# Attention with two heads on the halves of TensorE's columns and scaling on GpSimd, and a reordered end of each recurrence head

## The reference, cut to what matters

```python
# attention: 8 heads of 64, the tokens as rows of 64; a query sees 8 rows of keys (4 in the short sequence)
s = jnp.einsum('rqhd,rjkhd->hrqjk', qg, kg) * scale + bias       # bias: table by distance, -1e30 outside a 16 wide band
p = jax.nn.softmax(s.reshape(H, rows, GRID_W, kh * GRID_W), axis=-1)
o = jnp.einsum('hrqjk,rjkhd->rqhd', p, vg)

# recurrence: 4 heads of 128, forward and backward, the same for both
k, log_f = (1 - lb) * sigmoid(-z), log(max(lb + (1 - lb) * sigmoid(z), 1e-30))
S[t] = exp(log_f[t]) * S[t-1] + k[t] v[t]^T ;   o[t] = silu(q[t]) S[t]
```

## Time and profile before

| | us |
|---|---|
| median of 3 runs (lowest to highest) | 3038.07 (3037.3 to 3043.27) |
| the profiled execution, its own time | 3038.7 |
| its span | 3036.9 |
| attention, start of the first product to the end of the last copy | 484.7 to 639.2 |
| recurrence, closing products of the four heads begin at | 773.4, 868.9, 962.0, 1043.9 |

### The profile page before, as it was taken

One profiled execution on the slowest core, in us unless ns is written; L12 is line 12 of the kernel. 1 busy time (PEld: TensorE's weight loads), 2 busy tenths in 40 slices (PEclk: granted clock), 3 DMA queues, 4 the chain that ended last, 5 costly groups with the idle time before them and its releaser, 6 DMA issues. The chain is left out here.

```text
span 3036.9 us, 50700 instructions
## 1 busy us (share of the span) xinstructions
PE 2887.0 (95%) x19594; PEld 2707.7 (89%) x19594; DVE 2109.2 (69%) x3534; ACT 1577.8 (52%) x2728; POOL 549.4 (18%) x518
## 2 busy tenths in 40 slices
PE   7999999989988889978999999999999999999997
PEld 5888888978877778858999999999999999999997
DVE  7212224767888576677778877887788778778887
ACT  2111214654455333316666666666666666667774
POOL 2000110014534243311001100110011001102132
PEclk9999999999999989988999999999999999999998
DMA  6478864845545464328878887888788879889894
GB/s 225 157 212 253 271 187 117 237 171 192 193 168 192 141 216 135 125 97 273 255 259 267 266 258 258 268 263 257 256 273 259 257 257 285 262 255 313 273 298 142
DMA packets 534559, 686.64 MB, mean 226 GB/s; under 512 B 18969, under 2 KB 460584, under 8 KB 529200
## 3 DMA queue, kind: packets, MB, share of 16 engines
q1 hardware_dynamic: 514816, 627.96, 63.9%
q0 software_dynamic: 19504, 55.44, 7.0%
HBM read 577.46 MB, written 105.88 MB: 225 GB/s over the span
## 5 line engine op out<-in xcount | busy, mean ns | idle before, releaser
L2581 DVE TENSOR_TENSOR moe_low<-pieces_ring,moe_high 128x1024 fp32r<-128x1024 f32 x768 | 930.4, 1222 | 155.2 <-ACT moe_high L2484 154.5
L2484 ACT ACTIVATE moe_high<-pieces_ring 128x1024 fp32r<-128x1024 f32 x768 | 796.1, 1052 | 16.6 <-PEq L103 16.6
L2431 PE MATMUL moe_down<-moe_hdn,moe_high 128*128 128x320 f32 x1920 | 510.7, 346 | 9.6 <-DVE moe_outT_p L2619 4.3
L2431 PE MATMUL moe_gate<-moe_xT,moe_high 128*128 128x320 f32 x1792 | 480.8, 344 | 0.9 <-DVE moe_xT L2586 0.9
L2431 PE MATMUL moe_up<-moe_xT,moe_high 128*128 128x320 f32 x1792 | 474.0, 340 | 2.4 <-DVE moe_low L2581 2.4
L2432 PE MATMUL moe_down<-moe_hdn,moe_low 128*128 128x160 f32 x1920 | 453.4, 236 | 0.0
L2432 PE MATMUL moe_up<-moe_xT,moe_low 128*128 128x160 f32 x1792 | 423.4, 236 | 0.0
L2432 PE MATMUL moe_gate<-moe_xT,moe_low 128*128 128x160 f32 x1792 | 423.3, 236 | 0.0
L2431 PEld LDWEIGHTS moe_down<-moe_hdn,moe_high 128*128 128x128 f32 x1920 | 361.4, 188 | 17.8 <-DVE moe_hdn L2610 8.3
L2432 PEld LDWEIGHTS moe_down<-moe_hdn,moe_low 128*128 128x128 f32 x1920 | 366.9, 191 | 0.0
L2432 PEld LDWEIGHTS moe_gate<-moe_xT,moe_low 128*128 128x128 f32 x1792 | 343.0, 191 | 0.0
(11 more groups left out here) (344 smaller groups left out, 6075.0 us busy)
## 6 DMA issues: line engine op xcount, KB each, us to landing
pieces_ring<-in_w_gate_e SPq DMA_DIRECT2D x128, 1024.0 KB
pieces_ring<-in_w_up_e SPq DMA_DIRECT2D x128, 1024.0 KB
pieces_ring<-in_w_down_e SPq DMA_DIRECT2D x128, 1024.0 KB
bias_fx<-xs SPq DMA_DIRECT2D x40, 1024.0 KB, 5.3
fr_raw<-in_w_in SPq DMA_DIRECT2D x16, 1024.0 KB, 8.6
ws<-fr_late_split SPq DMA_DIRECT2D x32, 512.0 KB, 4.6
bias_fw<-ws SPq DMA_DIRECT2D x32, 512.0 KB, 8.2
mo_gates<-h SPq DMA_DIRECT2D x20, 512.0 KB, 4.5
```

What stands on the lines that cost most here:

```text
L2431: nc.tensor.matmul(ps[:, 0:2 * TOK], hi, x, start=(first and k == 0), stop=False)
L2484: nc.scalar.activation(high[:, g % HI, cols], ring[:, g % RAW, cols], ACT.Copy)\
L2581: nc.vector.tensor_tensor(low[:, g % HI, cols], ring[:, g % RAW, cols], high[:, g % HI, cols].bitcast(F32), ALU.subtract).then_inc(lo_done, 1)
```

## The change

In the attention, `values` takes both heads of a tile at once: for each chunk a product of 64 columns of `v` for head 0 into rows 0 to 63 of the result, and one for head 1 into rows 64 to 127. The two are addressed to the two halves of the array's columns, and one copy of 128 rows takes both out. The products of a tile are spread over two rounds, half the chunks in each. The scaling by the reciprocal goes from DVE to POOL. The turned tile is held in two buffers and copied in two parts, the first three chunks by ACT and the rest by DVE. `pT` has four slots instead of two. POOL makes the `na_inner` tables of the last two pairs of heads between scalings, and stores there as well. The pipeline is one round deeper.

In the recurrence the closing products wait for A group by group, the last `gather` stands ahead of `run_sums` on DVE, `gates` moves from round 6 to round 7, and in the first three heads the second half fill of the last level goes behind the closing products.

```diff
+                def scale(g):                                     # POOL
+                    keys, n = items[g][5], g % SLOTS
+                    pool.wait_ge(inverted, g + 1)
+                    nc.gpsimd.tensor_scalar(sc[:, n, 0:keys], sc[:, n, 0:keys], inv[:, n:n + 1], None, ALU.mult)\
+                      .then_inc(normed, 1)
+                make_inner(0)
+                make_inner(1)
+                for g in range(G):
+                    scale(g)
+                    pool.wait_ge(normed, g + 1)
+                    hp, n = divmod(g, N)
+                    if n == 2 and 1 <= hp < NA_HEADS // 2 - 1:
+                        make_inner(hp + 1)
+                    if n == 12 and hp >= 1:
+                        store(hp - 1)
...
-                    for c in range(0, keys, P):
-                        last = nc.tensor.matmul(o_ps[g % 2][:, 0:P], v[:, w, k0 + c // P, :], pT[:, g % 2, c:c + P],
-                                                start=(c == 0), stop=(c + P >= keys))
+                    for n in range(*((0, chunks // 2) if half == 0 else (chunks // 2, chunks))):
+                        for u in range(2):
+                            head = slice(u * NA_DIM, (u + 1) * NA_DIM)
+                            last = nc.tensor.matmul(o_ps[slot][head, :], v[:, w, k0 + n, head],
+                                                    pT[:, (2 * pair + u) % SLOTS, n * P:(n + 1) * P],
+                                                    start=(n == 0), stop=(n == chunks - 1))
...
-                for g in range(G + 4):
+                for g in range(G + 5):
                     if g < G:
                         scores(g)
                     if 3 <= g < G + 3:
                         turn(g - 3)
-                    if g >= 4:
-                        values(g - 4)
+                    if g >= 5:
+                        values((g - 5) // 2, (g - 5) % 2)
...
                     if g < G:                                     # DVE
                         bias(g)
-                    if 2 <= g < G + 2:
-                        norm(g - 2)
-                    if g >= 5:
-                        copy_o(g - 5)
+                    if 1 <= g < G + 1:
+                        invert(g - 1)
+                    if 3 <= g < G + 3:
+                        copy_p(g - 3)
+                    if g >= 7 and g % 2:
+                        copy_o((g - 7) // 2)
...
+            if hd + 1 < HG_HEADS:
+                points[-1] = (hd, "closed")
...
-                    pe.wait_ge(a_done, (hd + 1) * NL * NG)
                     pe.wait_ge(s_made, (hd + 1) * NS)
                     for g, (a, count) in enumerate(CHUNK_GROUPS):
+                        pe.wait_ge(a_done, ((hd + 1) * NL - 1) * NG + g + 1)
...
+                    fill((hd, "closed"))
...
-                        if r == 6 and hd + 1 < HG_HEADS:
+                        if r == 7 and hd + 1 < HG_HEADS:
                             gates(hd + 1, 1 - w)
...
+                    gather(R - 2)
                     if hd + 1 < HG_HEADS:
                         run_sums(hd + 1)
-                    gather(R - 2)
```

More of the change, by code:

```diff
@@ L721, in _ @@
-                for g in range(G + 4):
+                    for m, cols in enumerate(parts_of(g)):
+                        if g >= 1:
+                            pe.wait_ge(p_copied[m], g)
+                        for c in range(cols.start, cols.stop, P):
+                            last = nc.tensor.transpose(t_ps[m][:, c - cols.start:c - cols.start + P],
+                                                       sc[:, g % SLOTS, c:c + P], ident[:])
+                        last.then_inc(p_turned[m], 1)
@@ new lines, in values @@
+                def values(pair, half):
+                    hp, _, _, t, k0, keys, row, two = items[2 * pair]
+                    w, slot = hp % 2, pair % 2
+                    if half == 0:
+                        for m in range(2):
+                            pe.wait_ge(p_copied[m], 2 * pair + 2)
+                        if pair % PAIRS == 0:
+                            pe.wait_ge(v_in[w], 16 * (hp // 2 + 1))
+                        if pair >= 2:
+                            pe.wait_ge(o_copied, pair - 1)
+                    chunks = -(-keys // P)
+                    for n in range(*((0, chunks // 2) if half == 0 else (chunks // 2, chunks))):
[4 more added lines that the diff above has]
+                                                    start=(n == 0), stop=(n == chunks - 1))
+                    if half == 1:
+                        last.then_inc(pv_done, 1)
@@ L737, in bias @@
                     if g >= SLOTS:
-                        dve.wait_ge(p_turned, g - SLOTS + 1)
-                    rows = inner[:, 2 * hp + u] if two else table[:, 2 * hp + u, row:row + keys // GRID_W, :]
+                        dve.wait_ge(p_turned[1], g - SLOTS + 1)
+                    rows = inner[:, (2 * hp + u) % HEADS] if two else table[:, 2 * hp + u, row:row + keys // GRID_W, :]
                     nc.vector.tensor_tensor_reduce(
@@ L743, in bias, with invert @@
                         ALU.add, ALU.min, nmax[:, n:n + 1]).then_inc(biased, 1)
-                def norm(g):
-                    keys, n = items[g][5], g % SLOTS
+                def invert(g):
+                    n = g % SLOTS
                     dve.wait_ge(exp_done, g + 1)
[L748 to L752, removed]
```

96 lines of the change are left out of this document (50 added, 46 removed).

## The result

The changed kernel takes 3024.21 us (median of 5 runs, 3022.08 to 3025.53) against 3039.27 us (5 runs, 3037.3 to 3044.64) of the kernel before: ratio 0.9945, 95% interval 0.9931 to 0.9960, faster by 15 us. The forecast was 3001, with a range of 2986 to 3036. The sign is right, and less than half of the gain came.

What follows compares the result with a forecast made beforehand. PE was taken to bound the attention, while in the recurrence neither engine is full. From 3038.7 us, minus 30 (attention) and minus 7 (recurrence), with mixing and experts 0, gave 3001.7, stated as 3001; range 2986 to 3036.

Steps and rivals of the forecast that it cites:

- Value products, minus 35.5 us: Attention, PE: the two heads' products run at once on two column halves, two sharing one 0.111 us slot; minus 35.5 us.
- Switches of shape, taken at 0: Attention, PE: 160 switches between full and half width, two each way per round or fewer, assumed to cost about 0.
- the row of the 32-column transposes: Profile row before the change: 32-column transposes between full-width instructions, read as a switch at about 0.
- upper end of 0.166 us: Attention: if PE empties first, a switch costs a small product's length less its pitch, 0.166 us, 26.6 us in all.
- The forecast's sum for it with overlap, 3028 us: Attention: halves overlap but PE empties at each of 160 switches; 3001.7 + 26.6 = 3028 us.
- the forecast's first rival: Attention: halves overlap, but part of a drain, POOL or the chain through four slots takes over; 137 to 149 us, 3020; chance 0.26.
- Scaling on POOL at 1.0 us: Attention: a scaling of 512 to 576 columns takes about 1.0 us on POOL, ends 0.6 and 1.8; some 76 us for 80.
- 125: Attention's forecast length: 155.3 - 35.5 + 2 (DVE) + 2 (POOL) + 1.5 (pipeline) = 125 us, gain 30.
- DVE and ACT, 94.7 and 36 us: Attention: DVE's busy time falls from 118.2 to 94.7 us, ACT's copies from 47.8 to about 36 us.
- the 2 us for short rounds: Attention: in 16 rounds with 256 keys only DVE needs 1.05 us against PE's 0.93; plus 2 us.
- Recurrence, minus 7: Recurrence: moved gates and freed closing, less the scans' later place, give 1 + 3 + 3 = 7 us over three heads.
- 2 to 3.5 us a head: Recurrence: gain from moving the gates one round later, of which the scans' later place takes 1.5 to 2 us back.

Runs made afterwards that it cites:

- the run in one half: Changed kernel with all value products writing rows 0 to 63, one head's chunks per round, two copies out on DVE: 3053.22 us, ratio 1.0043 to the kernel before.
- The added switches: Changed kernel with the value products of 64 rounds laid in two places, one between the transposes' parts, 124 more changes of shape: 3039.66 us.
- full width: Changed kernel with value products 128 columns wide, one head per round, no overlap and no switch, POOL still scaling: 3032.61 us.
- half the switches: Changed kernel with both halves of a pair's value products in one round, 80 switches instead of 160: 3022.77 us.
- the shared version: Changed kernel with a pair's value products in one round, and scaling of odd items on DVE, even ones on POOL: 3016.01 us.
- no scaling on POOL: Changed kernel with all scaling back on DVE, directly behind the reciprocal: 3018.55 us.
- half of both: Same run as the shared version: changed kernel, value products once per pair, every second item's scaling on DVE: 3016.01 us.

## Why the prediction was right in sign and wrong in size

*Value products, minus 35.5 us: right.* The pitch halved, 32.5 us went from between the instructions, and the run in one half shows that the overlap is what did it.

*Switches of shape, taken at 0: the step that failed.* The forecast took the row of the 32-column transposes, which shows no drain, over its own upper end of 0.166 us. In the trace the borders of the value products cost 30.9 - 11.6 = 19.3 us more, and 3.0 of the 35.5 didn't come between the instructions: 22.3 us for 152 borders, 0.15 us each. The stage as a whole says the same more roughly: 151.1 - 159.6 + 35.5 less 2 to 6.1 for POOL is 21 to 25 us. The added switches gave 0.15 as well, and so does the run in one half, which has switches and no overlap. It stood 181.6 - 163.5 = 18.1 us above full width, with 5.4 us less of other waits (5.0 for POOL and 1.5 for ACT there against 1.1), 23.5 us for 155 changes. So the upper end, a small product's length less its pitch, was nearly the price. The forecast's sum for it with overlap, 3028 us, lies within 4 of the result, and has the switches 4 us too dear. What came is the forecast's first rival, given 0.26: an attention of 137 to 149 us, counted to 640.0, where 146.8 was measured on that scale, by the first of the causes it names, the drain. The Trainium skill has a change of tiling mode drain TensorE (TensorEngine Tiling (Array Packing), Key Properties); the gaps of 0.17 us in this trace agree. The row that the forecast preferred stays what it was, a change at no price, but for 32 columns and transposes; why it was free there wasn't tried, and it was too far from 64 columns and products to carry 160 changes. That a drain is what fills the 0.15 us is argued from its length; shown is that the changes of shape cost it.

*Scaling on POOL at 1.0 us: too low.* It took 1.57 and 1.73 us for 512 and 576 columns, 120 us in sum against 76. The row of a scaling, 583 ns for 127 columns, was no bad start. What failed is the slope, 1.0 ns a column as of a copy: from 256 to 512 columns it measured (1567 - 927) / 256 = 2.5 ns. PE's direct loss stayed small all the same. The weight loads waited 6.1 us for POOL, but 4.1 for DVE's scaling before, so 2 us more, as forecast. The larger effect is the hidden one: with POOL's 129 us under PE's 142, half the switches could go without gain. Nor could 125 have come true. POOL's first scaling starts 3.5 us into the stage, its last ends 8.0 us before the next stage, and between them POOL is busy for 125.2 us. So even switches at no price leave an attention of some 137 us, an estimate from these rows, where the forecast's 125 is 129.3 on the same scale.

*DVE and ACT, 94.7 and 36 us: 89.1 and 35.9.* Near enough; neither held the stage, and the 2 us for short rounds weren't needed: no wait for DVE is longer than 0.2 us.

*Recurrence, minus 7: minus 7.5 in the profile, 7 by the run of it alone.* The sum is right, and by luck, since its split is not. The level-7 wait in the second head (some 5 us forecast, 5.4 measured), closing at once behind the gather (forecast 214.7 us after the recurrence's start, measured 212.1), and PE's wait that moves to the next head's transposes came as described. But the whole gain hangs on the gates: put back, they cost 8.5 us, where the forecast had 2 to 3.5 us a head less what the later scans take. The kernel is then 8.2 us faster than before, what the attention gives alone, so for the gather ahead of the scans and the moved half fill together next to nothing is left; the scans put back cost 1.5 us, not to be told from none, and the half fill wasn't tried alone. The reason in the rows: the next head's first weights, done at 862.1 in the second head, hold PE's transposes at 862.6 whatever closing does before them; taking ACT's copies out of the way gave only 0.5 us a border.

*Left open.* The single steps of the recurrence sum to 10 us and the whole to 7; the difference is about what such runs can tell. What the shared version's 4.9 us without a releaser are isn't known.

## What to carry to other kernels

Narrow products pay if both halves of the columns get work, and each way into and out of the narrow shape is paid, here with 0.15 us on average: eight of these instructions save 0.44 us and lose 0.24 to 0.3. So it should pay to gather many in one place before switching; here that gave nothing while POOL did all the scaling. When work moves to a quiet engine, set its whole sum, at a slope from the same kind of instruction, beside the new time of the engine that it relieves. Test two suspects together and not only one at a time: half the switches gave nothing in the attention, no scaling on POOL 3.8 us, half of both 7.1. In the times that is weaker (1, 5.5 and 7 us, each with some us of doubt), and how the two are combined matters more: half the switches with all scaling on DVE was slower than either alone.

## What the runs showed of the hardware

DVE's scaling of 512 and 576 columns took 487 and 521 ns alone and, in the shared version, 747 and 817 ns on average where POOL scaled beside it, while POOL's went from 1567 to 1617 and from 1728 to 1806 ns. Behind these averages are two cases. Each of the 32 DVE scalings starts while one of POOL's is running. In 23 of them DVE's ends 0.28 us (512 columns) or 0.31 to 0.32 us (576) after POOL's has ended, however early it started, as in the first pair of rows. In the other 9 DVE's takes its 0.49 or 0.52 us as if alone and POOL's is 0.12 to 0.29 us longer, as in the second pair.

```profile
564.35 1.57 POOL L696 TENSOR_SCALAR na_sc<-na_sc,na_inv 128x512 f32<-128x512 f32 x1 [1.34 <-DVE na_inv L799]
565.32 0.87 DVE L803 TENSOR_SCALAR na_sc<-na_sc,na_inv 128x512 f32<-128x512 f32 x1
567.33 2.02 POOL L696 TENSOR_SCALAR na_sc<-na_sc,na_inv 128x576 f32<-128x576 f32 x1 [1.41 <-DVE na_inv L799]
568.30 0.52 DVE L803 TENSOR_SCALAR na_sc<-na_sc,na_inv 128x576 f32<-128x576 f32 x1
```

The Trainium skill has VectorE or GpSimd block the other for a whole instruction when both need the port pair that they share (SBUF — State Buffer, Terms, the shared port pair). The 23 agree: DVE is held until POOL's scaling is over. The 9 don't: DVE started 0.8 to 1.0 us behind POOL's and wasn't held. What decides between the two isn't known.

After the 6 us in which PE stood still in the second head, its first products ran at 1.2 GHz (granted clock 0.50), and at 2.4 again 5 us later. This isn't new: in the kernel before, the clock was at 0.50 from 868.9 to 874.4, after the wait ahead of closing. The stretches of the changed kernel, columns as before:

```profile
862.60:867.60 5.00, 5.00 (x24) 5.00 (x25) 5.00 (x3) 3.29 (x6) 3.00 (x2) 0.50 0.69 189
867.70:870.50 2.80, 2.80 (x28) 2.80 (x27) 2.59 (x3) 1.01 (x1) 2.64 (x2) 1.00 1.00 397
```
